# All sixteen late up tiles of each feed-forward stage by seven half products, and the KV norm's spread one unit later

## The reference

```python
def swiglu(h, w1, w3, w2):
    return (jax.nn.silu(h @ w1) * (h @ w3)) @ w2
...
        x = x + 0.5 * rms_norm(swiglu(rms_norm(x, g[0]), ffn_w1[l, 0], ffn_w3[l, 0], ffn_w2[l, 0]), g[1])
        hn = rms_norm(x, g[2])
...
        x = x + rms_norm(mix, g[3])
        x = x + 0.5 * rms_norm(swiglu(rms_norm(x, g[4]), ffn_w1[l, 1], ffn_w3[l, 1], ffn_w2[l, 1]), g[5])
        if l == N_A_LAYERS - 1:
            k_nope, k_rope, v_sh = mla_shared_kv(x, kv_in_norm, w_dkv_kr, kv_norm, w_ukv, cos_r, sin_r)
```

## Time and profile before

| | us |
|---|---|
| median of 3 runs (1943.36 to 1948.18) | 1947.6 |
| the profiled execution, device time | 1946.04 |
| its span, first to last instruction | 1943.8 |
| tensor engine (PE) busy | 1892.5 (97%) |
| weight loads (PEld, beside PE) | 1703.8 (88%) |
| vector engine (DVE) busy | 1269.6 (65%) |
| scalar engine (ACT) busy | 828.2 (43%) |
| GpSimd (POOL) busy | 48.6 (3%) |

### The profile page before, as it was taken

How to read it: one execution, slowest core, us unless ns; L and a number is a source line. 1 busy time by engine, 2 the same in 40 slices (tenths; PEclk the granted TensorE clock), 3 DMA queues, 4 the chain that set the end, 5 groups by cost and what they waited for, 6 DMA issues and landing times.

```text
span 1943.8 us, 28855 instructions
## 1 busy us (share of the span) xinstructions
PE 1892.5 (97%) x11693; PEld 1703.8 (88%) x11693; DVE 1269.6 (65%) x1742; ACT 828.2 (43%) x1203; POOL 48.6 (3%) x55
## 2 busy tenths in 40 slices
PE   8999999999999999999999999999988999999998
PEld 7899988978889899988987999889877898999887
DVE  5888752576757888862378887524766488877523
ACT  5444342455536444342354433423554464343422
POOL 0000000011100000000000000000000000000000
PEclk9999999999999999999999999999999999999999
DMA  5333333322213323343333333333211222333331
GB/s 164 87 109 108 103 104 97 87 66 76 76 55 88 107 82 106 96 119 90 91 80 87 101 95 108 102 107 81 59 33 55 65 76 79 107 108 106 109 89 44
DMA packets 347398, 175.09 MB, mean 90 GB/s; under 512 B 18478, under 2 KB 346268, under 8 KB 347292
## 3 DMA queue, kind: packets, MB, share of 16 engines
q1 hardware_dynamic: 346528, 172.51, 31.7%
q10 hardware_dynamic: 764, 1.11, 0.2%
HBM read 171.50 MB, written 2.10 MB: 89 GB/s over the span
## 4 chain that ended last, share of the span: by engine, by line
PE 87%; DVE 10%; ACT 1%; issue 1%; POOL 0%; DMA 0%; SPq 0%; DVEq 0%; ACTq 0%
PE acc L1762 22%; PE acc L1764 21%; PE acc L1763 21%; PE duo L1762 7%; PE duo L1763 7%; PE duo L1764 7%; DVE wl L1101 1%; DVE sqs L1212 1%; DVE y L1159 1%; DVE xT L1166 1%; PE duo L1790 1%; DVE xg L1136 1%; DVE hT L1402 1%; DVE mx L1460 1%; PE acc L2004 1%
## 5 line engine op out<-in xcount | busy, mean ns | idle before, releaser
L1762 PE MATMUL acc<-xg,wh 128*128 128x256 f32 (+1 forms) x1624 | 538.6, 332 | 6.2 <-DVE wl L1101 2.7
L1763 PE MATMUL acc<-xg,wh 128*128 128x256 f32 (+1 forms) x1624 | 532.1, 328 | 0.0
L1764 PE MATMUL acc<-xg,wl 128*128 128x256 f32 (+1 forms) x1624 | 531.7, 327 | 0.0
L1762 PEld LDWEIGHTS acc<-xg,wh 128*128 128x128 f32 x1624 | 310.3, 191 | 36.0 <-DVE wl L1101 3.1
L1763 PEld LDWEIGHTS acc<-xg,wh 128*128 128x128 f32 x1624 | 310.4, 191 | 26.9 <-issue 1.4
L1764 PEld LDWEIGHTS acc<-xg,wl 128*128 128x128 f32 x1624 | 310.3, 191 | 26.3
L1101 DVE TENSOR_TENSOR wl<-raw,wh 128x1024 fp32r<-128x1024 f32 (+2 forms) x204 | 235.0, 1165 | 136.0 <-ACT wh L632 135.1
L1762 PE MATMUL acc<-hT,wh 128*128 128x512 f32 (+1 forms) x704 | 255.7, 363 | 3.5 <-DVE wl L1101 3.5
L1763 PE MATMUL acc<-hT,wh 128*128 128x512 f32 (+1 forms) x704 | 255.2, 363 | 0.0
L1764 PE MATMUL acc<-hT,wl 128*128 128x512 f32 (+1 forms) x704 | 255.2, 363 | 0.0
L632 ACT ACTIVATE wh<-raw 128x1024 fp32r<-128x1024 f32 (+2 forms) x204 | 200.5, 1009 | 126.5 <-PE acc L1764 80.6
(11 more groups left out here) (263 smaller groups left out, 3150.4 us busy)
## 6 DMA issues: line engine op xcount, KB each, us to landing
raw<-in_ffn_w_dram SPq DMA_DIRECT2D x240, 512.0 KB, 4.5
raw<-in_ffn_w_dram SPq DMA_DIRECT2D x32, 384.0 KB, 3.5
raw<-in_moba_w_qkv_dram SPq DMA_DIRECT2D x24, 512.0 KB, 3.9
raw<-in_moba_w_o_dram SPq DMA_DIRECT2D x8, 512.0 KB, 4.1
raw<-in_mla_w_o_dram SPq DMA_DIRECT2D x8, 512.0 KB, 4.1
xin<-in_x_dram SPq DMA_DIRECT2D x4, 512.0 KB, 5.6
raw<-in_mla_w_dq_dram SPq DMA_DIRECT2D x4, 512.0 KB, 4.1
raw<-in_mla_w_uq_dram SPq DMA_DIRECT2D x8, 256.0 KB, 2.9
```

Of the source, the lines that this page charges most:

```text
L1762: t.matmul(dst, w_h, m_h, start=start, stop=False)
L1763: t.matmul(dst, w_h, m_l, start=False, stop=False)
L1764: return t.matmul(dst, w_l, m_h, start=False, stop=stop)
```

## The change

Full tiles are gone: tiles 6 to 21 are all made by seven products. `turn` becomes `fast`, one tile; a loop turn is two tiles (the two slot pairs), with tiles 6 and 7 ahead of the loop on the tensor engine and tiles 20 and 21 behind it on ACT and DVE. The loops start at 8 on the tensor engine and SP (7 turns) and at 6 on ACT and DVE (7 turns). The fifth `x_part` goes. The last tile now needs second sum and rows, which are put among the splits of the hidden tiles and of the first down weights, whose order changes. In the KV stage the spread moves from before unit 7 to before unit 8; DVE makes the variance behind tile 2, and the diagonal behind the splits of units 8 and 9; ACT copies x for the products behind the copies of weight units 6 and 7; DVE empties tile 2's first bank ahead of the x products and scales the latent behind the splits of units 10 and 11. The plain units from 4 on all wait for `r + i - 3` results.

```diff
-    FS, TURN, KH = 6, 4, KD // 2
-    FAST_U = [(UT, 1), (UT, 1), (UT + KH, 0)]
-    TURN_U = FAST_U * (TURN - 1) + [(UT, 1)] * 2
-    TURNS, GT = (KF - FS) // TURN, TURN - 1
-    FFN_U = [(UT, 1)] * (2 * FS) + TURN_U * TURNS + [(n, 1) for n in DOWN] * KD
+    FS, KH = 6, KD // 2
+    FAST = KF - FS
+    FFN_U = [(UT, 1)] * (2 * FS) + [(UT, 1), (UT, 1), (UT + KH, 0), (0, 0)] * FAST + [(n, 1) for n in DOWN] * KD
...
-        return u + 2 * FS + len(TURN_U) * ((f - FS) // TURN) + len(FAST_U) * ((f - FS) % TURN)
+        return u + 2 * FS + 4 * (f - FS)
...
-                with sp.Fori(0, TURNS - 1) as it:
-                    for c in range(TURN):
-                        w = tile_unit(u0, FS + c)
-                        up(FS + 2 + TURN * it + c, c % 2, lambda a: read(len(TURN_U) * it + w))
-                for f in range(KF - 2, KF):
-                    up(f, f % 2, lambda a: read(tile_unit(u0, f - 2)))
+                with sp.Fori(FS // 2 + 1, KF // 2) as it:
+                    for j in range(2):
+                        up(2 * it + j, j, lambda a: read(tile_unit(u0, 2 * it + j - 2)))
...
-                    act.wait_ge(unit_done, u + SLOTS)
-                    x_full()
                 for f in range(2, FS - 1):
                     split(u + 2 * f + 2)
                     split(u + 2 * f + 3)
+                    if f == 2 and kv is not None:
+                        act.wait_ge(unit_done, u + SLOTS)
+                        x_full()
...
-                def turn(it, q=None):
...
-                turn(0, 0)
-                with act.Fori(1, TURNS - 1) as it:
-                    turn(it)
-                turn(TURNS - 1, TURNS - 1)
+                def first_product(f, j):
+                    act.wait_ge(prod_psum, 2 * (G0 + f - FS) + 1)
+                    s.activation(usum[:, 0], tile_banks(j)[0][:, half(0)], COPY).then_inc(m1_copied, 1)
+                def fast_gate(f):
+                    act.wait_ge(rows_ready, 2 * (G0 + f - FS) + 1)
...
+                def fast(f, j, count):
+                    w = tile_unit(u, f)
+                    first_product(f, j)
+                    for i in range(3):
+                        tile_hi(f + 1, i, 2 * (1 - j), count, w + (1, 2, 4)[i])
+                    fast_gate(f)
...
+                with act.Fori(FS // 2, KF // 2 - 1) as it:
+                    for j in range(2):
+                        fast(2 * it + j, j, count_of(FS + j + 1) + 16 * (it - FS // 2))
+                fast(KF - 2, 0, count_of(KF - 1))
...
-                act.wait_ge(unit_done, d0 - 2)
+                w, d0 = tile_unit(u, KF - 1), down_unit(u)
                 hidden_hi(0)
+                first_product(KF - 1, 1)
+                split(d0)
+                act.wait_ge(w_lo, d0)
                 hidden_hi(1)
-                act.wait_ge(unit_done, d0 - 1)
-                gate(KF - 1, tile_banks(KF - 1)[0][:])
-                split(d0)
+                split(d0 + 1)
+                act.wait_ge(unit_done, w + 2)
                 hidden_hi(2)
                 hidden_hi(3)
-                act.wait_ge(unit_done, d0)
-                split(d0 + 1)
+                act.wait_ge(unit_done, w + 4)
                 hidden_hi(4)
+                fast_gate(KF - 1)
+                hidden_hi(5)
                 split(d0 + 2)
-                hidden_hi(5)
                 split(d0 + 3)
                 hidden_hi(6)
...
+                if kv is not None:
+                    scaled(2, 0)
                 for k in range(0, KD, KH):
                     dve.wait_ge(xf_ready, KD * nth + k + KH)
                     v.tensor_tensor(xn[:, k:k + KH], xn[:, k:k + KH],
                                     Rb[:].unsqueeze(1).broadcast_to([P, KH, S]), ALU.mult).then_inc(xn_ready, 1)
-                plain(2)
+                if kv is None:
+                    scaled(2, 0)
+                scaled(2, 1)
+                plain_gated(2)
+                if kv is not None:
+                    norm_var(N_CKV)
+                split(u + 8)
+                split(u + 9)
                 if kv is not None:
                     between()
-                split(u + 8)
...
+                split(u + 10)
+                split(u + 11)
                 if kv is not None:
                     after()
-                split(u + 10)
...
-                def turn(it, q=None):
...
-                turn(0, 0)
-                with dve.Fori(1, TURNS - 1) as it:
-                    turn(it)
-                turn(TURNS - 1, TURNS - 1)
+                def fast(f, j, dst, counts):
+                    w, g, banks, slot = tile_unit(u, f), G0 + f - FS, tile_banks(j), 2 * (1 - j)
+                    outer_sums(w + 4, g + 1, slot, counts)
+                    tile_lo(w + 4, 0, slot)
+                    second_sum(g, banks)
+                    inner_sums(g + 1, slot)
+                    tile_lo(w + 4, 1, slot)
+                    rows(f, w, g, banks)
+                    tile_lo(w + 4, 2, slot)
+                    dve.wait_ge(rows_ready, 2 * g + 2)
+                    gated(f, dst, T[2][:])
+                with dve.Fori(FS // 2, KF // 2 - 1) as it:
+                    for j in range(2):
+                        fast(2 * it + j, j, hid[:, bass.ds(2 * it + j, 1)].rearrange("p a s -> p (a s)"),
+                             [c + 16 * (it - FS // 2) for c in counts_of(FS + j + 1)])
+                fast(KF - 2, 0, hid[:, KF - 2], counts_of(KF - 1))
...
-                d0 = down_unit(u)
+                f, d0 = KF - 1, down_unit(u)
+                w, g, banks = tile_unit(u, f), G0 + f - FS, tile_banks(1)
                 hidden_lo(0)
+                split(d0)
                 hidden_lo(1)
-                split(d0)
-                dve.wait_ge(unit_done, d0)
-                gated(KF - 1, hid[:, KF - 1], tile_banks(KF - 1)[1][:])
+                second_sum(g, banks)
+                split(d0 + 1)
                 hidden_lo(2)
+                rows(f, w, g, banks)
                 hidden_lo(3)
-                split(d0 + 1)
+                dve.wait_ge(rows_ready, 2 * g + 2)
+                gated(f, hid[:, f], T[2][:])
                 hidden_lo(4)
+                hidden_lo(5)
                 split(d0 + 2)
-                hidden_lo(5)
                 split(d0 + 3)
                 hidden_lo(6)
...
-                norm_var(N_CKV)
                 norm_diag(N_CKV, 0, 1.0, ckv_diag)
...
-                    u, r, first = u + len(KV_U), r + KK + 1, 2
-                    for a in range(4):
-                        pe.wait_ge(evacuated, R0[st] + a + 1)
-                        if a == 2:
-                            mean(N_CKV, width=KVR)
-                        if a == 3:
-                            spread(N_CKV, diag=ckv_diag)
-                        unit(u + 4 + a, acc[a][:], from_x(xg))
-                for i in range(4 * first, 2 * FS - 1):
+                    u, r = u + len(KV_U), r + KK + 1
+                for i in range(SLOTS, 2 * FS - 1):
                     pe.wait_ge(evacuated, r + i - 3)
+                    if st == KV_ST and i == 6:
+                        mean(N_CKV, width=KVR)
+                    if st == KV_ST and i == 8:
+                        spread(N_CKV, diag=ckv_diag)
                     unit(u + i, acc[i % 4][:], from_x(xg))
...
-                def turn(it, q=None):
...
-                        pe.wait_ge(hid_ready, KF * nth + f - 1)
-                        pe.wait_ge(w_lo, w + 1)
...
-                turn(0, 0)
-                with pe.Fori(1, TURNS) as it:
-                    turn(it)
+                def fast(f, j, first=False):
+                    w, g = tile_unit(u, f), FAST * nth + f - FS
...
+                    pe.wait_ge(hid_ready, KF * nth + f - 1)
+                    pe.wait_ge(w_lo, w + 1)
+                    x_wait(xb_lo, 1)
+                    tiles(sums[:, half(0)], 0, 0, KH, quarter(0, 0)).then_inc(prod_psum, 1)
+                    x_wait(xb_lo, 3)
+                    tiles(pairs[:, half(0)], 0, KH, KH, quarter(1, 0)).then_inc(unit_done, 1)
+                    pe.wait_ge(w_lo, w + 2)
+                    x_wait(tx_lo, 2)
+                    tiles(rest[:, HALF:2 * HALF], 1, 0, KH, xsum(0))
+                    tiles(rest[:, 0:HALF], 1, KH, KH, xsum(1)).then_inc(unit_done, 1)
+                    pe.wait_ge(w_lo, w + 4)
+                    x_wait(tx_lo, 4)
+                    pe.wait_ge(m1_copied, g + 1)
+                    tiles(sums[:, half(1)], 2, 0, KH, xsum(2)).then_inc(prod_psum, 1)
+                    x_wait(xb_lo, 4)
+                    tiles(pairs[:, half(1)], 2, KH, KH, quarter(1, 1))
+                    tiles(rest[:, 2 * HALF:3 * HALF], 3, 0, KH, xsum(3)).then_inc(unit_done, 2)
+                for j in range(2):
+                    fast(FS + j, j, j == 0)
+                with pe.Fori(FS // 2 + 1, KF // 2) as it:
+                    for j in range(2):
+                        fast(2 * it + j, j)
```

148 lines of the change are left out of this document (32 added, 116 removed).

## The result

| | before | changed |
|---|---|---|
| median, us | 1945.48 (4 runs, 1943.19 to 1948.18) | 1927.08 (4 runs, 1924.97 to 1929.56) |
| the profiled execution, us | 1946.04 | 1924.97 |
| its span, us | 1943.8 | 1922.8 |

The account below looks back on a forecast made before the run. Tensor engine bounds the kernel (97% busy), vector engine a close second. -13.1 - 4.2 + 0.6 = -16.7 us from the profiled 1946.0 gives 1929.3; with the median 1.6 above it, 1931; range 1926 to 1937.

Parts of the forecast that it names:

- Full tiles become seven products: Up tiles, tensor engine: 16 full tiles fall from 10.90 to 10.08 us each, 13.1 us less.
- The vector engine follows at no cost: Seven-product tiles: 9.55 to 9.63 us of vector work fits in 10.08, about 0.5 us to spare per tile.
- upper end of 10.12: Seven-product tile: the vector engine's time in us if a steady stream lost the overlap between its operations.
- (a): Rival, up tiles: vector engine partly sets the pace at 10.12 to 10.2 us a tile, 1934 to 1939 us; chance 0.06.
- (e): Rival, up tiles: vector engine never catches up; gain gone from 10.35 us a tile, 1958 us at 10.5; chance 0.03.
- Loads, loop ends, the fifth x part at nothing: Feed-forward stages: unchanged loads, more backward branches and the dropped x split were each costed at nothing.
- rival (d): Loop ends: added branches stall on instruction fetch, costing 8 to 21 us, so 1939 to 1952 us; chance 0.02.
- The down projection, +0.6 us: First down projection of each stage: hole moves from step 8 to 16 and grows 0.15 us, four times.
- Rival (b): Down projection: the hole takes the added vector work whole, 1940 us; chance 0.03.
- The KV norm, 4.2 us: Shared KV norm: the wait before the spread goes, gaining 3.9 to 4.4 us, 4.2 taken; spread costs 0.5 to 0.95.
- Rival (c): KV norm: the wait is only moved, 1935 us; chance 0.02.
- I cost the clock at nothing: Tensor engine clock: granted 1.00 in stretches read, and the change makes no idle stretch, so no cost.

Follow-up runs that it names:

- experiment 1: The kernel before with only the KV norm's new order, full tiles kept: 1939.81 us, ratio 0.9958 to the kernel before.
- experiment 7: The changed kernel with an unread 512-column vector multiplication at the end of each seven-product tile's list: 1929.47 us, ratio 0.9907 to the kernel before.
- experiment 9: The changed kernel with an unread vector reduction over 896 columns in every seven-product tile from 6 to 20: 1954.18 us, ratio 1.0026 to the kernel before.
- experiment 3: The changed kernel with the 768-column weight split moved ahead of the sixth hidden group: 1923.32 us, ratio 0.9872 to the kernel before.
- experiment 2: The changed kernel with the old KV order, so the tile change alone: 1934.66 us, ratio 0.9930 to the kernel before.
- experiment 5: The kernel before with 17 unread matmuls ahead of the waiting KV spread: 1944.79 us against 1948.70 for the kernel before, ratio 0.9981.

## Why the prediction was right, and where it was not

- **Full tiles become seven products, 13.1 us: right.** Stages 1, 2 and 4 got 3.28, 3.28 and 3.29 us shorter, and the third 3.23 with experiment 1's 4.06 for the KV part taken off: 13.1 in all. The clean lengths of both kinds of tile stood in the trace, so the difference was exact. The 19.0 that the prediction works out from the isolated gap in the Trainium skill, page "TensorE: Matmul & The Clock Gate", section on the back-to-back issue gap, is not what this stream gave.
- **The vector engine follows at no cost: right, its margin too small.** 9.45 us of work and 0.63 to spare (experiment 7), where I had 9.6 and about 0.5. I took only the marked idle time off, which is less than what the wait costs, and inside the loop there is unmarked waiting too. Two other terms were off without touching the time: the engine's extra work is 93 us, not 16 x 3 (the full tile's 6.58 us leave out what the tile ahead of it was spared: 7.14 us busy from 147.68 to 157.76 in the kernel before), and eight operations of a tile overlap the next in the earlier trace rows's stretch, not six or seven. The upper end of 10.12 and rivals (a) and (e) needed work that isn't there; experiment 9 shows the price where it is, and fits the order of the break-even of 10.35.
- **Loads, loop ends, the fifth x part at nothing: right.** Every stage's up tiles are shorter by four differences of tile lengths (4 x 0.82 = 3.28), with nothing left for branches, so rival (d) is out.
- **The down projection, +0.6 us: right.** The hole moved to step 16 as laid out and the first three projections grew by 0.13 to 0.17 each. In parts it went a little otherwise: the hole itself is 1.06, not 1.2, so it grew by 0.02 only, and the other tenth of a us is spread over other steps of the first result tile in amounts of a few hundredths (0.06 at step 14, which the prediction had as perhaps late). Rival (b) is out. What I didn't see is that swapping two entries of the list would have removed the hole (experiment 3, 4.8 us).
- **The KV norm, 4.2 us: right for the hole.** 4.01 to 4.06 in the trace, with 0.88 left for the spread, within the 0.5 to 0.95 of the prediction. Rival (c) is out.
- **"I cost the clock at nothing": this step failed.** The argument was that nothing in the change makes an idle stretch. It didn't ask what becomes of the idle stretch that the change removes. Its price had a second part, the slow matmuls behind it at half clock: 2.5 us in experiment 2's trace, nothing in before's profiled execution, from which the sum was worked out. On the mean over executions it is 3.7 us (1.9 to 5.5, experiment 5); with it the sum is 20.4, and both comparisons hold it. The 1.6 us by which the median of before lay above its profiled execution was carried over whole for the same reason; how much of it belonged to the KV place isn't shown. That the range still holds the median is thus partly luck: its lower end was argued from the down hole and the KV wait alone.

How often the clock falls behind a given hole isn't settled: the mean clocks in experiment 5 point to most executions at the KV place, but only one profile of each run's kernel shows where it fell, and none why.

## What to carry to other kernels

Where the trace of before has a clean stretch of either kind, the difference of two start-to-start distances predicts a swap of kinds to a few hundredths of a us; a margin, though, is best measured by adding work until the tile grows, since idle marks leave waits out. A hole of the tensor engine costs its length and, in some executions, slow matmuls behind it, so a sum against one profiled execution should be given with that part as a range. Where a hole can't be removed, matmuls that nobody reads took the second part away here, at the KV place and in the attention blocks.
